# x read a second time in 32x32 blocks and turned by VectorE, in place of TensorE's transposes of x

## The reference, cut to what matters

```python
def first_block(x, mem, ...):
    mem_n = rms_norm(mem, norm_mem_g)
    h = rms_norm(x, norm_in_g[layer])
    proj = jnp.einsum('bsd,de->bse', h, w_in[layer])          # 256 x 2048 by 2048 x 17408
    (qa, ka, va, za, qb, kb, vb, zb, qm, zm, gates) = jnp.split(proj, split_points, axis=-1)
    ya = moba_attention(rope(qa), rope(ka), va) * silu(za)    # 8 heads of 128
    yb = dilated_mixture(rope(qb), rope(kb), vb) * silu(zb)   # 3 groups of 4 heads
    mk, mv = jnp.split(jnp.einsum('bmd,de->bme', mem_n, w_mem_kv[layer]), 2, axis=-1)
    ym = memory_attention(qm, mk, mv) * silu(zm)              # 4 heads of 256
    merged = g_a * (ya @ w_proj_a) + g_b * (yb @ w_proj_b) + g_m * (ym @ w_proj_m)
    x = x + merged @ w_out
    return rms_norm(x, norm_final_g)
# second_block: x + w_out2(RG-LRU of 1024 channels | retention of 8 heads), then a gated feed-forward, and a last norm
```

## Time and profile before

| | us |
|---|---|
| median of 3 runs | 2211.49 (2210.34 to 2211.49) |
| the profiled execution, its own time | 2209.47 |
| its span, from first to last instruction | 2207.5 |
| TensorE busy | 2188.8 (99%) |
| VectorE busy | 1322.6 (60%) |
| ScalarE busy | 1022.3 (46%) |
| GpSimd busy | 132.5 (6%) |

### The profile page before, as it was taken

One profiled execution on the slowest core, in us unless ns is written; L12 is line 12 of the kernel. 1 busy time (PEld: TensorE's weight loads), 2 busy tenths in 40 slices (PEclk: granted clock), 3 DMA queues, 4 the chain that ended last, 5 costly groups with the idle time before them and its releaser, 6 DMA issues.

```text
span 2207.5 us, 26246 instructions
## 1 busy us (share of the span) xinstructions
PE 2188.8 (99%) x9938; PEld 1813.1 (82%) x9938; DVE 1322.6 (60%) x1661; ACT 1022.3 (46%) x1227; POOL 132.5 (6%) x222
## 2 busy tenths in 40 slices
PE   8999999999999999999999999999999999999998
PEld 7888888888888888888888888888888888888886
DVE  5655656676455645546676888665555555554454
ACT  5544444444444444444555655454444444444443
POOL 0010101011000000000111000110001000100000
PEclk9999999999999999999999999999999999999999
DMA  8775656567654657667777554577777777776664
GB/s 289 220 228 175 206 166 213 183 224 244 204 162 145 218 172 232 204 213 274 235 253 241 189 169 162 192 238 213 214 211 225 217 214 210 227 236 192 193 195 147
DMA packets 227328, 460.45 MB, mean 209 GB/s; under 512 B 16024, under 2 KB 16288, under 8 KB 226336
## 3 DMA queue, kind: packets, MB, share of 16 engines
q1 hardware_dynamic: 212128, 408.73, 59.5%
q0 software_dynamic: 14368, 49.30, 7.3%
q10 hardware_dynamic: 736, 1.12, 0.1%
HBM read 435.49 MB, written 23.59 MB: 208 GB/s over the span
## 4 chain that ended last, share of the span: by engine, by line
PE 89%; DVE 6%; ACT 2%; DMA 1%; issue 1%; POOL 0%; SPq 0%; POOLq 0%; ACTq 0%; DVEq 0%
PE ps L1488 29%; PE ps L1490 29%; PE ps L1489 29%; DVE w_lo L859 2%; ACT w_hi L571 1%; PE ps L1380 1%; PE ps L1349 1%; PE ps L1402 1%; DMA raw<-in_w_in 0%; DVE tmp L1015 0%; DMA raw<-in_w_out 0%; DVE stage L1010 0%; DMA raw<-in_w_mem_kv 0%; DVE tmp L1028 0%; PE ps L1391 0%
## 5 line engine op out<-in xcount | busy, mean ns | idle before, releaser
L859 DVE TENSOR_TENSOR w_lo<-raw,w_hi 128x1024 fp32r<-128x1024 f32 (+1 forms) x776 | 931.3, 1211 | 766.4 <-ACT w_hi L571 764.1
L571 ACT ACTIVATE w_hi<-raw 128x1024 fp32r<-128x1024 f32 (+1 forms) x776 | 809.9, 1050 | 899.8 <-PE ps L1490 821.7
L1488 PE MATMUL ps<-w_hi,xT_hi 128*128 128x512 f32 x1088 | 429.9, 395 | 0.2 <-DVE w_lo L859 0.2
L1490 PE MATMUL ps<-w_hi,xT_lo 128*128 128x512 f32 x1088 | 424.1, 390 | 0.0
L1489 PE MATMUL ps<-w_lo,xT_hi 128*128 128x512 f32 x1088 | 423.6, 389 | 0.0
L1488 PE MATMUL ps<-w_hi,u2T_hi 128*128 128x512 f32 x704 | 273.9, 389 | 0.0
L1490 PE MATMUL ps<-w_hi,u2T_lo 128*128 128x512 f32 x704 | 273.9, 389 | 0.0
L1489 PE MATMUL ps<-w_lo,u2T_hi 128*128 128x512 f32 x704 | 273.9, 389 | 0.0
L1490 PEld LDWEIGHTS ps<-w_hi,xT_lo 128*128 128x128 f32 x1088 | 204.2, 188 | 43.4
L1488 PEld LDWEIGHTS ps<-w_hi,xT_hi 128*128 128x128 f32 x1088 | 204.4, 188 | 42.0 <-DVE w_lo L859 1.1
L1489 PEld LDWEIGHTS ps<-w_lo,xT_hi 128*128 128x128 f32 x1088 | 204.5, 188 | 40.8
(11 more groups left out here) (264 smaller groups left out, 2274.6 us busy)
## 6 DMA issues: line engine op xcount, KB each, us to landing
raw<-in_w_in SPq DMA_DIRECT2D x368, 512.0 KB, 4.5
raw<-in_w_ffn_gate SPq DMA_DIRECT2D x88, 512.0 KB, 3.8
raw<-in_w_ffn_up SPq DMA_DIRECT2D x88, 512.0 KB, 4.4
raw<-in_w_ffn_down SPq DMA_DIRECT2D x88, 512.0 KB, 4.6
raw<-in_w_out SPq DMA_DIRECT2D x64, 512.0 KB, 4.9
bounce<-tmp POOLq DMA_DIRECT2D x37, 512.0 KB, 3.3
stage<-bounce POOLq DMA_DIRECT2D x148, 128.0 KB, 5.2
raw<-in_w_mem_kv SPq DMA_DIRECT2D x32, 512.0 KB, 5.6
```

The source lines that it names most:

```text
L571: nc.scalar.activation(w_hi[:, s, 0:per], raw[:, s, 0:per], ACT.Copy).then_inc(hi_ready, 1)
L859: nc.vector.tensor_tensor(w_lo[:, s, 0:per], raw[:, s, 0:per], w_hi[:, s, 0:per].bitcast(F32), ALU.subtract)\
L1488: nc.tensor.matmul(bank(2 * par + t), x_hi, w_hi[:, s, k], start=first, stop=False)
L1490: ins = nc.tensor.matmul(bank(2 * par + t), x_lo, w_hi[:, s, k], start=False, stop=last)
```

## The change

x is read from memory a second time, by GpSimd's queue, into a new tile `xb_in` (16 KiB a partition), in 64 DMAs of 32 partitions by 8 runs of 32 numbers (128 B): four quarters of 16. The blocks land in the places that they have in the transposed x, each one not yet turned. VectorE turns the 32 x 32 blocks with two transposes of 128 x 512 per quarter into `xb_T` (two buffers, `x_turn`), ScalarE makes `xT_hi` from it (`x_hi`) and VectorE `xT_lo` (`x_lo`). TensorE's four jobs for x are gone; it waits instead for `x_lo_made` at chunks 0, 2, 4 and 6 of the first tile of w_in. The first read of x into `x_tok` stays, for the sums of squares. The turns are behind chunk 6 of the third tile and chunks 3 and 7 of the fourth, and chunk 2 of the first tile of w_in; `x_factors` moves from chunk 1 to chunk 2 of the third tile. On GpSimd quarter 0 is issued behind carry 1, quarter 1 behind the root of x, and quarters 2 and 3 behind carry 2. `jobs`, `job` and their waits for mem stay as they are.

```diff
@@ -151,6 +151,8 @@
         zm = at("zm", [P, NT, 1024], F32, 144)
         mv = at("mv", [P, NT, 1024], F32, 152)
         mkT = at("mkT", [P, 8, S], F32, 160)
+        xb_in = at("xb_in", [P, KC * S], F32, 168)
+        xb_T = [at(f"xb_T{k}", [P, QUAD * S], F32, 136 + 4 * k) for k in range(2)]
         half_at = (120, 160)
         qaT, kaT, va, za = (
             [at(f"{n}{h}", s, F32, half_at[h] + 4 * m) for h in range(2)]
@@ -266,6 +268,8 @@
             sem(n) for n in ("in_const", "in_vec", "in_res", "in_g1", "in_dec", "in_gw", "in_g2"))
         spilled, in_h2, stored = sem("spilled"), sem("in_h2"), sem("stored")
         x_added, row_made = sem("x_added"), sem("row_made")
+        in_xb = [sem(f"in_xb{q}") for q in range(QUAD)]
+        xb_turned, x_hi_made, x_lo_made = (sem(n) for n in ("xb_turned", "x_hi_made", "x_lo_made"))
         t0_done, t0_hi, t0_lo = (sem(n) for n in ("t0_done", "t0_hi", "t0_lo"))
         acc_done, rows_added, rows_sq, rows_mean, rows_root, rows_scaled = (
             sem(n) for n in ("acc_done", "rows_added", "rows_sq", "rows_mean", "rows_root", "rows_scaled"))
@@ -518,10 +522,24 @@
                         pool.dma_start(stage[32 * m:32 * (m + 1), :, :].rearrange("p t (q x) -> p t q x", q=4),
                                        bounce.rearrange("(q a) (t m x) -> m a t q x", a=32, t=NT, m=4)[m]).then_inc(b_in, 16)
 
+            def load_x_blocks(q):
+
+
+                rows = x.rearrange("(u a) (c m b) -> c m a u b", a=32, m=4, b=32)
+                for c in range(q * QUAD, (q + 1) * QUAD):
+                    for m in range(4):
+                        pool.dma_start(xb_in[32 * m:32 * (m + 1), c * S:(c + 1) * S].rearrange("p (u b) -> p u b", b=32), rows[c][m])\
+                            .then_inc(in_xb[q], 16)
+
             norm_root(0, R["mem"]["r"])
             carry(1, 1)
+            load_x_blocks(0)
             norm_root(1, R["x"]["r"])
-            carry(2, 17)
+            load_x_blocks(1)
+            carry(2, 2)
+            load_x_blocks(2)
+            load_x_blocks(3)
+            carry(3, 17)
             pool.wait_ge(w_used, G_X + SLOTS)
             for t in range(NT):
                 pool.dma_start(x1[:, t], x[t * P:(t + 1) * P, :]).then_inc(in_res, 16)
@@ -780,10 +798,16 @@
                                     6: [mem_in, lambda: squares(mem_tok, sumsq_m, lambda t: None)]}
             four[1]["act_hooks"] = {7: [lambda: act.wait_ge(b_out, 16),
                                         lambda: squares(x_tok, sumsq_x, lambda t: act.wait_ge(in_x[t], 16 * QUAD))]}
-            for n in (2, 3):
-                four[n]["act_hooks"] = {6: jobs(xT_hi, V_IN, 2 * n - 4), 7: jobs(xT_hi, V_IN, 2 * n - 3)}
-            last = four[3]["act_hooks"].pop(7)
-            four[3]["act_hooks"][5] = [log_sigmoid_exp]
+            def x_hi(q):
+                act.wait_ge(xb_turned, q + 1)
+                for c in range(QUAD):
+                    kc = q * QUAD + c
+                    ins = nc.scalar.activation(xT_hi[:, kc], xb_T[q % 2][:, c * S:(c + 1) * S], ACT.Copy,
+                                               scale=cols[:, V_IN + kc:V_IN + kc + 1])
+                ins.then_inc(x_hi_made, 1)
+
+            four[2]["act_hooks"] = {7: [lambda: x_hi(0)]}
+            four[3]["act_hooks"] = {4: [lambda: x_hi(1)], 5: [log_sigmoid_exp]}
             act.dma_start(vec_a[:, :], vecs[0:P]).then_inc(in_vec, 16)
             act.dma_start(vec_b[0:V_END - P, :], vecs[P:V_END]).then_inc(in_vec, 16)
             act.wait_ge(pool_c, 1)
@@ -805,7 +829,7 @@
             four[0]["act_hooks"][0] = [second_half]
             prev = chain(four, None)
             tiles = tiles_attention()
-            tiles[0]["act_hooks"] = {1: last}
+            tiles[0]["act_hooks"] = {0: [lambda: x_hi(2)], 3: [lambda: x_hi(3)]}
             prev = chain(tiles, prev)
             prev = chain(tiles_merge(0, first=True), prev)
             w.rounds(act, NG - 1, lambda i: chain(tiles_merge(i + 1), merge_last(i)))
@@ -1280,15 +1304,29 @@
 
             four[0]["dve_hooks"] = {0: [second_half], 1: jobs(memT_hi, memT_lo, V_MEM, 1), 3: jobs(memT_hi, memT_lo, V_MEM, 2),
                                     5: jobs(memT_hi, memT_lo, V_MEM, 3), 7: [mem_factors]}
-            for n in (2, 3):
-                four[n]["dve_hooks"] = {6: jobs(xT_hi, xT_lo, V_IN, 2 * n - 4), 7: jobs(xT_hi, xT_lo, V_IN, 2 * n - 3)}
-            last = four[3]["dve_hooks"].pop(7)
-            four[2]["dve_hooks"][1] = [x_factors]
+            def x_turn(q):
+                dve.wait_ge(in_xb[q], 16 * 4 * QUAD)
+                for k in range(2):
+                    c = slice(k * NW, (k + 1) * NW)
+                    ins = nc.vector.transpose(xb_T[q % 2][:, c], xb_in[:, q * QUAD * S + k * NW:q * QUAD * S + (k + 1) * NW])
+                ins.then_inc(xb_turned, 1)
+
+            def x_lo(q):
+                dve.wait_ge(x_hi_made, q + 1)
+                for c in range(QUAD):
+                    kc = q * QUAD + c
+                    ins = nc.vector.scalar_tensor_tensor(xT_lo[:, kc], xb_T[q % 2][:, c * S:(c + 1) * S],
+                                                         cols[:, V_IN + kc:V_IN + kc + 1], xT_hi[:, kc].bitcast(F32),
+                                                         ALU.mult, ALU.subtract)
+                ins.then_inc(x_lo_made, 1)
+
+            four[2]["dve_hooks"] = {2: [x_factors], 6: [lambda: x_turn(0)]}
+            four[3]["dve_hooks"] = {0: [lambda: x_lo(0)], 3: [lambda: x_turn(1)], 5: [lambda: x_lo(1)], 7: [lambda: x_turn(2)]}
             first_lo(t0_hi, range(2), t0_lo)
             prev = chain(four, None)
             log_sigmoid()
             tiles = tiles_attention()
-            tiles[0]["dve_hooks"] = {1: last}
+            tiles[0]["dve_hooks"] = {1: [lambda: x_lo(2)], 2: [lambda: x_turn(3)], 4: [lambda: x_lo(3)]}
             prev = chain(tiles, prev)
             prev = chain(tiles_merge(0, first=True), prev)
             w.rounds(dve, NG - 1, lambda i: chain(tiles_merge(i + 1), merge_last(i)))
@@ -1569,13 +1607,9 @@
             four = tiles_memkv()
             begin(four[0], mem_tok, in_mem)
             four[0]["need"][0].append(lambda: pe.wait_ge(cols_ready, 1))
-            for n in (2, 3):
-                four[n]["pe_hooks"] = {k: [lambda q=q: job(q, x_tok, in_x)] for k, q in ((2, 2 * (n - 2)), (4, 2 * (n - 2) + 1))}
             prev = chain(four, None)
             tiles = tiles_attention()
-            tiles[0]["need"] = {0: [lambda: pe.wait_ge(tx_free[0], w.n["j0"] - 1), lambda: pe.wait_ge(tx_free[1], w.n["j1"] - 1)],
-                                4: [lambda: pe.wait_ge(tx_free[0], w.n["j0"])],
-                                6: [lambda: pe.wait_ge(tx_free[1], w.n["j1"])]}
+            tiles[0]["need"] = {2 * q: [lambda q=q: pe.wait_ge(x_lo_made, q + 1)] for q in range(QUAD)}
             prev = chain(tiles, prev)
             tiles = tiles_merge(0, first=True)
             for k, units in ((3, 4), (4, 12), (5, 16)):
```

## The result

The changed kernel takes 2217.22 us (median of 16 runs, 2213.80 to 2220.47), the kernel before beside it 2211.78 (16 runs, 2209.59 to 2214.89). The ratio is 1.0025, with a 95% interval of 1.0019 to 1.0032: slower by 5.4 us, 0.25%. The forecast was 2214.8, the range 2209.5 to 2227.5. The profiled execution took 2216.6, with a span of 2214.7.

The account below looks back on a forecast made before the run. TensorE's stream of weight chunks was taken to bound the kernel. +1.5 (Step 1), +4.0 (Step 2), +0.3 (Step 3), +1.0 (Step 4) and -3.5 of transposes gave +3.3 on 2211.49: 2214.8 us, range 2209.5 to 2227.5.

Parts of the forecast that it names:

- no change that can be told: Whole kernel: the forecast case, +3.3 us, own range -1 to +6.4, under the 4.4 us that can be told; chance 0.47.
- the side "slower": Whole kernel: slower by more than 0.2% (4.4 us); chance 0.50, from 0.14 of the forecast, the backlog and 0.03.
- the backlog: GpSimd's queue: block DMAs take longer than the 0.61 us between issues, delaying the bounce; +16 us at 1.0 us each; chance 0.33.
- The bound of the gain: TensorE: 32 transposes of x in four groups removed, all on the chain, at most 3.5 us or 0.16%.
- Step 1: VectorE, third mem tile: x's factors behind chunk 2 make the w_lo of chunks 3 and 4 late, +1.5 us.
- Step 2: GpSimd's queue: two quarters' issues delay the second mkT, so TensorE waits 4.0 us at the fourth mem tile's chunk 2.
- Step 3: From there to w_in's first chunk: VectorE's work costs TensorE 0.3 us of waiting; quarters 2 and 3 hide.
- Step 4: DMA queues: the blocks' traffic beside the weights, 0.2 us of all engines per block DMA, makes the bounce 1 us later.
- the lower bound: DMA engines: if only bytes cost, a block DMA takes 0.14 us of all 16, against 0.57 if pieces cost the same.
- the bounce behind the blocks: GpSimd's queue: the bounce of M1's turned tile takes 1.0 us more than 4.2 to the first load.
- the upper end: Bounce to first load: 8.05 us as in the first carry in a full queue, +3.9 us.
- The hidden case: Fourth mem tile: the second mkT comes by 83.2 us, so the sum is -2.0, or -3.5 if Step 1 hides; chance 0.14.

Follow-up runs that it names:

- one_transpose: Kernel before with 28 of the 32 TensorE transposes of x left out, scalings kept; 2209.44 against 2210.98 us, ratio 0.9994.
- factors_c2: Kernel before with only the factors of x moved from chunk 1 to chunk 2 of the third tile; 2210.86 against 2210.98 us, ratio 0.9996.
- dma_alone: Kernel before, transposes kept, plus the 64 block DMAs in the changed kernel's places, never used, and x's factors behind chunk 2; 2220.35 against 2210.98 us.
- carry_first: Changed kernel with carrying M1's turned tile moved ahead of quarter 1's 16 block DMAs; 2215.76 us against 2210.98 for the kernel before, ratio 1.0015.
- fill: Changed kernel with 22 unused matmuls on TensorE in the wait before the fourth tile's chunk 2; 2216.13 us against 2210.54 for the kernel before.
- sp_queue: spread2 with the 64 block DMAs on SyncE's queue, four behind each chunk of mem's last two tiles; 2213.88 us against 2210.54 for the kernel before.
- spread3: spread2 with the logarithm moved into w_in's fourth tile and quarter 1's turn behind chunk 5; 2209.10 us against 2210.42 for the kernel before.
- spread2: Changed kernel with block DMAs spread over GpSimd's idle stretches, x's factors back behind chunk 1, later turns moved; 2211.72 us against 2210.54 for the kernel before.

## Why the prediction was right

The sign, the place and the mechanism came out, and the size in part by luck. The likeliest single case was no change that can be told, at +3.3 us; the side "slower" had 0.50 only because the backlog brought 0.33 of it, and a backlog of that size did not happen. By the prediction's steps:

- **The bound of the gain**, 3.5 us of transposes: one_transpose gives 3.2 for 28 of 32, so some 3.7 for all. Right.
- **Step 1**, +1.5 us: 1.1 us in the changed kernel, and nothing of it in the end, since M3 c2 waits for something later. The prediction said so ("only the 90.5 counts"). Alone it is nothing (factors_c2).
- **Step 2**, GpSimd's queue: issues of 0.58 in place of 0.61 us, the bounce at 71.7 in a trace whose M0 c1 is 1.4 us earlier, so 73.1 against the predicted 73.6. The wait of TensorE is 5.1 to 5.8 us against 4.0 and 1.0 for the traffic. dma_alone shows the cause alone, carry_first that the line's place makes it. Shown. The copy of mkT stands at 88.4 against 88.3 (87.3 and the 1.0), and that is luck: the bounce took 2.8 us more than the 5.2 that the prediction gave it, and from the first load to the copy it was 7.2 us (79.79 to 86.98) in place of 9.5. The four loads had less beside them: in those 7.2 us the weights' queue moved 0.85 MB, in the 9.5 us of the kernel before 2.22 MB. That this made them faster is argued, not shown.
- **Step 3**: no wait at A0 c0 in the changed kernel, against 0.3. Right. It is there as soon as the turns come later (carry_first).
- **Step 4**, the blocks' cost in the queues. The queues from 58 to 68 us in the changed kernel (packets, MB, share of 16 engines):

```profile
q1 hardware_dynamic: 1020, 1.97, 68.5%
q0 software_dynamic: 520, 0.53, 22.1%
...
xb_in<-in_x POOLq DMA_DIRECT2D x14, 32.0 KB, 3.3
```

  520 packets of data and semaphores with 22.1% of 16 engines over 10 us are 68 ns a packet, against 190 for the four loads. With 14 to 16 DMAs in the stretch that is some 32 packets and 0.14 us of all engines for one, the lower bound. A block DMA lands 3.3 us after its issue here, and none of the 64 takes more than 7.3: no backlog as in the rival, with landings over 15 us.

- **The term that was mis-sized**: the bounce behind the blocks, 1.0 us in the sum. From its issue to the first load it took 8.05 us against 4.23 before, 3.8 more, the upper end that the prediction had from the first carry. The trace shows why. The software queue behind the bounce's issue, in the changed kernel from 71.74 to 76.4 us and in the kernel before from 67.16 to 70.5 us:

```profile
q0 software_dynamic: 113, 0.12, 19.1%
...
q0 software_dynamic: 143, 0.52, 43.8%
```

  Before, the whole bounce (0.52 MB) is moved in these 3.3 us, and its first packet starts 1.2 us after the issue. In the changed kernel the queue first moves what is left of the blocks, 0.12 MB, and the bounce's first packet starts 4.7 us after its issue. GpSimd had issued the 32 block DMAs, but the last of them were not yet carried out: the twelfth to the sixteenth of the second burst land 3.9, 4.1, 5.6, 5.7 and 6.6 us after their issue. All four traces with the burst right ahead of the bounce are alike: first packet after 4.7 to 4.9 us, first load after 8.05 and 9.3 (changed kernel), 9.3 (dma_alone) and 9.7 us (fill). Where the bounce stands elsewhere it is 3.6 to 4.7 us in seven traces. In two it is 6.5 and 6.3 (one_transpose, without block DMAs, and sp_queue, with them on the other queue); there the first packet starts after 1.2 and 1.6 us and the last ones come late. So 3.5 us are the bounce's stand behind blocks that were late themselves. Their own cost is not what made them late: 19.1% of 16 engines over 4.66 us is 0.9 us. What did, and what held those two other bounces, is open.
- **The missed term**: TensorE's clock. No step priced a half clock behind a wait. Against the mean of the two traces before, M3 c2 is 4.8 us late; two groups of transposes less give back 1.7 behind it, and the half clock takes 2.8: +5.9, as measured. In the second trace it is 5.3, 1.7 and 1.9: +5.5. Without the half clock the change would have stayed under the 4.4 us of what can be told, by this count; fill, which kept the clock, did not show that in time.

The rivals: the backlog of 12.8 us and more did not happen, since pieces of 128 B cost in proportion to their bytes; a bounce behind blocks that are still to be carried out did, with 3.5 us. The rule in the Trainium skill ("DMA: Bandwidth & Descriptors", Specifications) that pieces under 512 B miss line rate would have put a block DMA at the upper bound; the trace does not agree in this place, with 0.14 us in place of 0.57. The hidden case did not happen either. The rule in the Trainium skill on VectorE's two ports ("SBUF — State Buffer", "SBUF: two separate sides") was not seen to cost anything: the turn of quarter 0 at 70.73 runs beside the last two issues of the burst that takes 9.25 us, no more than the first one's 9.31 without a turn beside it. And in dma_alone, which has no turns, the bounce is no faster (9.3 us to the first load).

**What stays open.** In time, one_transpose and spread3 gain 1.5 and 1.3 us, in the stretch 3.2 and 2.9. Behind A0 c1 their traces are 2094.5 and 2094.6 us long, those of the kernel before 2090.9 and 2093.6. Whether an earlier TensorE gives time back later, in waits for raw and for turned keys, or whether this is scatter of 2 to 3 us, these runs can't tell.

## What to carry to other kernels

When DMAs are added to a queue that also carries a hand-over between engines, sum the issues that stand ahead of it, and add what is issued but not yet carried out (3.5 us here): 32 x 0.58 us of issues from 51 us on became a wait of TensorE at 85 us, through a copy on ScalarE that nobody had touched. Put such issues where the queue is idle, and then look for the next instruction with no lead (here the logarithm before A0 c0). Price a wait of TensorE not by its length alone: one of 5.1 us cost 2.8 us more in slow matmuls, one of 5.8 us in the same kernel 1.9 us more.

## What the hardware showed that was not expected

- Waits of 5.1 and 5.8 us (changed kernel), 5.1 (dma_alone), 2.7 (carry_first) and 2.6 us (sp_queue) came with a granted clock of 0.50 for 3.4 to 6.8 us, in the wait's last part or behind it; behind 0.6 us (before) and 1.7 us (spread2) it stayed at 1.00. With matmuls in the wait (fill) it stayed at 1.00.
- DMA pieces of 128 B, 8 to a partition, read from memory by the software queue: 0.14 us of all 16 engines for 32 KB, a quarter of what 128 KB in the four loads took (0.57), and 0.58 us to issue beside their 0.61.
- The first packet of the bounce started 4.7 to 4.9 us after its issue where it stood right behind 16 block DMAs, the last of which were issued and not yet carried out, and 1.2 us after it in the kernel before.
- The same 512 KB write of the bounce buffer took between 3.6 and 9.7 us from its issue to the load behind it, in one stretch of kernels that differ little.
